# A hybrid recurrent trunk on one core: late norm scale, grouped last units, moved output slices, transposed scan outputs

## What is computed

```python
def rmsnorm(x, w):
    return x * rsqrt(mean(x * x) + EPS) * w
def swiglu(h, wg, wu, wd):
    return (silu(h @ wg) * (h @ wu)) @ wd
# state space scan of a chunk, for head r of group g
acs = cumsum(ac)
lmat = where(causal, exp(acs_i - acs_j), 0)
y = einsum('bijg,bijgr,bjgrp->bigrp', c @ b.T, lmat, xs * dt)
y = y + einsum('bign,bgrpn->bigrp', cc, S) * exp(acs)
S = S * exp(acs[-1]) + einsum('bjgn,bjgr,bjgrp->bgrpn', bc, exp(acs[-1] - acs), xs * dt)
y = y + xs * d_skip
```

## Time and profile before

| | |
|---|---|
| median of three runs | 3383.99 us (3383.58 to 3386.05) |
| the profiled execution | 3374.13 us |
| its span | 3372.3 us |
| TensorE busy | 3171.9 us, 94% |
| VectorE, ScalarE, GpSimd busy | 1592.2, 782.3, 1006.2 us |
| mean granted clock of TensorE | 0.987 of 2.4 GHz |

### The profile page before, as it was taken

How to read it: one execution, slowest core, us unless ns; L and a number is a source line. 1 busy time by engine, 2 the same in 40 slices (tenths; PEclk the granted TensorE clock), 3 DMA queues, 4 the chain that set the end, 5 groups by cost and what they waited for, 6 DMA issues and landing times.

```text
span 3372.3 us, 46391 instructions
## 1 busy us (share of the span) xinstructions
PE 3171.9 (94%) x20050; PEld 3047.4 (90%) x20050; DVE 1592.2 (47%) x1899; ACT 782.3 (23%) x1115; POOL 1006.2 (30%) x528
## 2 busy tenths in 40 slices
PE   6999899999799999999897999999978999999997
PEld 5999898888699999999887998989968999999997
DVE  5344647557632222221467858678686221222224
ACT  4222413414410000000134324143244100000002
POOL 2222211201023333332324535344441332333331
PEclk9999999999899999999999999999999999999998
DMA  4111100101011111111112223131220111111111
GB/s 144 65 64 59 53 26 26 46 26 33 20 50 44 51 44 50 44 44 51 39 43 94 79 78 108 57 107 66 88 91 27 53 49 46 44 51 44 51 44 63
DMA packets 79240, 190.79 MB, mean 57 GB/s; under 512 B 20900, under 2 KB 36932, under 8 KB 78920
## 3 DMA queue, kind: packets, MB, share of 16 engines
q1 hardware_dynamic: 52384, 150.03, 13.1%
q10 hardware_dynamic: 26664, 37.88, 3.5%
HBM read 164.07 MB, written 19.59 MB: 54 GB/s over the span
## 4 chain that ended last, share of the span: by engine, by line
PE 82%; DVE 11%; ACT 3%; issue 2%; DMA 1%; ACTq 0%; SPq 0%; DVEq 0%
PE ps_set L555 68%; PE ps_core L815 4%; PE ps_set L564 3%; ACT work L1073 2%; DVE work L1597 2%; PE ps_core L1010 2%; ACT L1073 1%; DVE work L1916 1%; DVE h_lo L1583 1%; PE ps_core L1015 1%; DVE work L1807 1%; DVE work L2127 1%; PE ps_core L1005 1%; DVE work L2079 1%; DMA x<-in_x 1%
## 5 line engine op out<-in xcount | busy, mean ns | idle before, releaser
L481 POOL CAST w_hi<-w_raw 128x1024 fp32r<-128x1024 f32 x230 | 260.0, 1130 | 2185.7 <-PE ps_set L555 1949.9
L555 PE MATMUL ps_set<-h_hi,w_hi 128*128 128x344 f32 x3696 | 812.5, 328 | 14.6 <-ACT work L1073 14.5
L555 PE MATMUL ps_set<-h_lo,w_hi 128*128 128x344 f32 x3696 | 784.5, 320 | 0.0
L555 PE MATMUL ps_set<-h_hi,w_lo 128*128 128x344 f32 x3696 | 780.9, 320 | 0.0
L555 PEld LDWEIGHTS ps_set<-h_hi,w_hi 128*128 128x128 f32 x3696 | 620.6, 188 | 37.7 <-issue 17.1
L555 PEld LDWEIGHTS ps_set<-h_lo,w_hi 128*128 128x128 f32 x3696 | 625.2, 189 | 0.0
L555 PEld LDWEIGHTS ps_set<-h_hi,w_lo 128*128 128x128 f32 x3696 | 616.7, 188 | 0.0
L484 POOL TENSOR_TENSOR w_lo<-w_raw,w_hi 128x1024 fp32r<-128x1024 f32 x230 | 597.8, 2599 | 18.4
L2014 DVE TENSOR_TENSOR work<-work,ps_set 128x1032 f32<-128x1032 f32 x44 | 54.1, 1229 | 816.2 <-PE ps_set L555 806.3
L1672 DVE TENSOR_TENSOR x<-x,ps_set 128x1032 f32<-128x1032 f32 x160 | 196.7, 1229 | 256.4 <-PE ps_set L555 256.4
L1073 ACT ACTIVATE work<-ps_set 128x1032 f32<-128x1032 f32 x116 | 120.1, 1035 | 721.5 <-PE ps_set L555 695.0
(11 more groups left out here) (224 smaller groups left out, 3427.8 us busy)
## 6 DMA issues: line engine op xcount, KB each, us to landing
w_raw<-in_w SPq DMA_DIRECT2D x230, 512.0 KB, 3.3
work<-ssm_cum_rows ACTq DMA_DIRECT2D x32, 512.0 KB, 4.1
sample<-in_ssm_state SPq DMA_DIRECT2D x16, 512.0 KB, 4.0
out_ssm_s<-sample SPq DMA_DIRECT2D x16, 512.0 KB, 2.6
x<-in_x SPq DMA_DIRECT2D x6, 688.0 KB, 14.8
work<-work ACTq DMA_DIRECT2D x16, 258.0 KB, 2.4
out_y<-x SPq DMA_DIRECT2D x6, 688.0 KB, 3.4
sample<-bc_rows SPq DMA_DIRECT2D x8, 512.0 KB, 4.8
```

Source lines behind the costliest of these rows:

```text
L481: return nc.gpsimd.tensor_copy(w_hi[:, k, :], w_raw[:, k, :])
L555: mm = nc.tensor.matmul(out[:, g, 0:TN], w[:, slot, cols], v[:, g * TN:(g + 1) * TN], start=(start and n == 0), stop=(stop and n == 2))
```

## The change

Four changes stand in one kernel.

1. Norms 1 and 3 give x times w without the root. VectorE multiplies the gate by the root as it leaves PSUM, ScalarE takes its Silu, VectorE multiplies that by the root again (for the up side) and then with the up unit. The mean squares move behind projections.
2. Tile B of every pair is multiplied, copied and subtracted by token groups, and the last up unit of each feed-forward part is projected by groups.
3. In the last delta head, seven of eight output slices of the head before, and the additions to x, move from the levels to ahead of u and into the recurrence.
4. In the scan y comes out channels by tokens: the operands of yc and y are swapped, so that the y products have 64 columns of weights and write one half of the partitions each. The factor exp(cum) is then a row by tokens (`ECUM`), broadcast by two more DMAs of ScalarE for a chunk and exponentiated there. Both scalings of x read PSUM (dt goes into KDEC once). The product is added to the carried part, then D times x (`skip`). The transposes of y go.

```diff
@@ boundary on TensorE
+                if n in (1, 3):
+                    for g in range(TG):
+                        outputs_of(g)
+                    projections(0)
+                    mean_square(0)
+                    projections(1)
+                    mean_square(1)
+                    projections(2, lambda: mean_square(2))
+                    return
@@ gated_delta on TensorE
-                fill(out, 1)
+                fill(out, 0 if h + 1 == HEADS else 1)
+
+                late = h + 1 == HEADS
...
-                        fill(out, 1)
+                        if not late:
+                            fill(out, 1)
...
+                if late:
+                    fill(out, 1)
                 pe.wait_ge(*gdn_dve.value(n("Nb")))
...
+                    if late and c < 6:
+                        fill(out, 1)
@@ ffn on TensorE
+                def by_group(jobs, job, turn, unit):
+                    part = take(jobs, job, turn)
+                    pe.wait_ge(w_split, unit + 1)
+                    for g in range(TG):
+                        for c in range(KC):
+                            mm = group_products(ps_set[part][:, g, :], unit % 2, c, (h_hi[:, c, :], h_lo[:, c, :]), g,
+                                                c == 0, c == KC - 1)
+                        mm.then_inc(*((unit_done, 1) if g == TG - 1 else (part_done, 1)))
@@ state_space on TensorE
-                        nc.tensor.matmul(ps_core[part][:, :], tok(5, c * P, c * P + P), work[:, 12, 0:512],
-                                         start=True, stop=True).then_inc(*ssm_pe.step(n(f"yc{c}")))
+                        for t in range(4):
+                            mm = nc.tensor.matmul(ps_core[part][:, t * P:(t + 1) * P], work[:, 12, t * P:(t + 1) * P],
+                                                  tok(5, c * P, c * P + P), start=True, stop=True)
+                        mm.then_inc(*ssm_pe.step(n(f"yc{c}")))
...
-                        mm = nc.tensor.matmul(ps_core[part][:, h * HD:(h + 1) * HD], SC_TILE[c % 2][:, h],
-                                              XDT[c % 2][:, h * HD:(h + 1) * HD], start=True, stop=True)
+                        lower = HD * (h % 2)
+                        mm = nc.tensor.matmul(ps_core[part][lower:lower + HD, h // 2 * P:(h // 2 + 1) * P],
+                                              XDT[c % 2][:, h * HD:(h + 1) * HD], SC_TILE[c % 2][:, h], start=True, stop=True)
...
-                    part = take(core, n(f"yt{c}"), 0, [n(f"y{c}")])
-                    for t in range(4):
-                        mm = nc.tensor.transpose(ps_core[part][:, t * P:(t + 1) * P], work[:, 11, t * P:(t + 1) * P], ident)
-                    mm.then_inc(*ssm_pe.step(n(f"yt{c}")))
@@ ScalarE
+                def products(g, first=0, last=KC):
+                    for c in range(first, last):
+                        if c % 2 == 0:
+                            act.wait_ge(*x_pair_ready(n, g, c // 2))
+                        fn(h_hi[:, c, span(g)], x[:, c, span(g)], ACT.Identity, scale=NORM_W[:, n, c:c + 1])\
+                            .then_inc(*norm_act[n].step(f"hi{c}.{g}"))
...
+                    fn(RSTD, RSTD, ACT.Exp, scale=-0.5).then_inc(*norm_act[n].step("rstd"))
...
+            def end_rows(c, gr):
+
+                if c > 2:
+                    act.wait_ge(*ssm_dve.value(f"acc{c - 2}.{gr}"))
+                heads = ssm_cum_rows[gr][c].rearrange("(t e n) -> t e n", e=2, n=P)
+                for e in range(2):
+                    act.dma_start(ECUM[c % 2][HD * e:HD * e + HD, :].rearrange("p (t n) -> p t n", n=P),
+                                  heads[:, e, :].unsqueeze(0).to_broadcast([HD, 4, P])).then_inc(ecum_in[c % 2], 16)
...
                     if c:
+                        end_rows(c, gr)
                         differences(c, gr)
                         decays(c, gr)
+                        act.wait_ge(ecum_in[c % 2], 32 * ((4 if c % 2 else 3) * gr + (c + 1) // 2))
+                        fn(ECUM[c % 2], ECUM[c % 2], ACT.Exp).then_inc(*ssm_act.step(n(f"ec{c}")))
@@ VectorE
+                if n == 1:
+                    for g in range(TG):
+                        for q in range(4):
+                            add(g, q)
+                    lows(0, 0, KC)
+                    lows(1, 0, KC)
+                    sums(0)
+                    lows(2, 0, KC)
+                    sums(1)
+                    sums(2)
+                    return
...
+                    v.tensor_tensor(grp(tok(c)), grp(RSTD), big(jobs.part(name)), ALU.mult).then_inc(jobs.sem(name), 1)
+                    dve.wait_ge(*ffn_act[m].value("silu" + "AB"[c], pair))
+                    v.tensor_tensor(tok(c), tok(c), RSTD, ALU.mult).then_inc(*ffn_dve[m].step("f" + "AB"[c]))
...
+                    if last and c < 6:
+                        add_before(c + 2)
...
+                    turned = heads8(ps_core[core.part(n(f"xt{c}"))][:, :])
+                    v.tensor_tensor(heads8(XDT[s]), turned, spread(dt, HD), ALU.mult)
+                    v.tensor_tensor(heads8(XDEC[s]), turned, spread(KDEC[:, c, mine], HD), ALU.mult)\
                         .then_inc(core.sem(n(f"xt{c}")), 1)
...
+                        end = ECUM[c % 2]
                         dve.wait_ge(*ssm_pe.value(n(f"yc{c}")))
...
+                        dve.wait_ge(*ssm_act.value(n(f"ec{c}")))
+                        v.tensor_tensor(end, end, ps_core[core.part(n(f"yc{c}"))][:, :], ALU.mult).then_inc(core.sem(n(f"yc{c}")), 1)
...
+                        v.tensor_tensor(end, end, ps_core[core.part(n(f"y{c}"))][:, :], ALU.add).then_inc(core.sem(n(f"y{c}")), 1)
...
+                    if c:
+                        dve.wait_ge(*core.read(n(f"y{c}")))
+                        skip(end).then_inc(*ssm_dve.step(n(f"acc{c}")))
```

More of the change, by code:

```diff
@@ new lines, in pair @@
+                def pair(i, k, last=False):
+                    unit = i * 12 + (base + 4 + 6 * k)
+                    count = i * 2 + (k + 1)
+                    gate(loop, f"ga.{k}", i, unit, 0, count, i * 2 + k)
+                    gated_a(loop, f"ua.{k}", i, unit + 1, count)
+                    add_outputs(loop, [f"out{t}.{k}" for t in range(KC)], i, unit + 2, i * 12 + (parts + 6 * k))
+                    low_a(count)
+                    gate(loop, f"gb.{k}", i, unit + 4, 1, count, i * 2 + k)
+                    gated_b(loop, f"ub.{k}", i, unit + 5, count, last)
```

228 lines of the change are left out of this document (152 added, 76 removed).

## The result

The changed kernel takes 3389.65 us (median of 20 runs, 3385.78 to 3396.78) where the kernel before, timed beside it, takes 3384.36 (20 runs, 3380.58 to 3387.63): ratio 1.0018, 95% interval 1.0011 to 1.0025. Slower by 5 us, where 3325.5 was predicted and 3297 to 3358 was the range.

The account below looks back on a forecast made before the run. TensorE was taken to bound the kernel, hardly waiting in the feed-forward loops, with idle time that could go in six places. 11 + 11 + 13 + 1.5 + 22 = 58.5 us off the median 3384.0 gave 3325.5 us, range 3297 to 3358.

Parts of the forecast that it names:

- Part 4: State space scan: without y transposes a chunk takes 9.1 us, 0.87 less; 22 us gained over four groups, ends 0 and 38.
- D times x 1.04: Scan, VectorE's work for a chunk: multiplying x by D and adding was put at 1.04 us.
- VectorE's ring: Scan: VectorE's chain of work from one yc to the next, 8.9 us a chunk, 9.2 with the sum over samples.
- Rival (a): Scan: its wait comes back in full because VectorE, stretched by GpSimd, needs 9.9 us a chunk; gain 36.5, 3347; chance 0.17.
- Rival (b): Scan: even and odd heads' y products run at once on array halves, y 1.0 us; 27 us more, 3298; chance 0.10.
- Part 1: Norms 1 and 3: projections start before the root is ready; 11 us gained at boundary 1 and 11 at boundary 3.
- the one load for both: Boundaries: one table set holding logarithm and exponential would give 2.6 us more; the sum kept the second load, 1.28 us.
- two bank waits cost 2 us: Boundary 3: VectorE's additions and lows beside the outputs make two bank waits costing 2 us; gain still 11 us.
- Part 2: Ends of both feed-forward parts: working by groups removes 4.7 us of wait and some 1.8 of low clock; 13 us together.
- Part 3: Last delta head: levels and the stretch ahead of u gain, recurrence loses 7.7 us; net gain 1.5 us, ends -6 and +7.
- rival (d): Scan: added broadcasts delay the row broadcast on ScalarE's queue; chunk 11.7 us, +56 for the scan, 3404; chance 0.03.
- ScalarE's ring: Scan: landing 4.1 us plus 3.5 us of differences and exponential, 7.6 us; covered except 1.5 us at the fourth chunk.

## Why the prediction was wrong

**Part 4, the step that failed.** "D times x 1.04" in VectorE's ring took the 341 ns of L2127 in the earlier trace rows, an instruction that reads PSUM, for one that reads SBUF twice. The two sizes are equal; the operand's place is not. It measured 1255 ns in 64 of 112, 58 us. The earlier trace rows had the warning: of the 128x512 instructions L2062 and L2105, both inputs in SBUF, took 988 and 1246 ns, and L2102, from PSUM, 689. I had even used that difference once, as a gain, for the second scaling, and didn't apply it to the edit that went the other way. How far this step reaches: with the sum in PSUM or one wide addition at the end the kernel gets 27 or 32 us back, of the 47 that lie between the forecast -22 and the measured +25. The new scan then gains 2 or 7 us over the old one (0.9939 or 0.9923 against 0.9944, with intervals that overlap), not 22. The rest is a bank held longer in the one, and waits that are left in the other; no run splits it further.

The Trainium skill (SBUF — State Buffer, Who interferes with whom) states the rule: a VectorE instruction with two SBUF inputs contends with a GpSimd instruction that reads SBUF, and whichever started first holds the shared ports for its whole length while the other is blocked. The trace agrees: each of four short instructions ends 0.14 or 0.15 us behind one of GpSimd's, as above, and with GpSimd idle each takes 0.34 us. I left this rule out of the prediction; it was the one that spoke against the change. An estimate from the traces' own durations (four instructions, each behind one of GpSimd's 2.4 to 2.7 us, in three chunks of eight) gives up to 10 us a chunk, tens of microseconds over the scans.

**Rival (a) was the nearest.** It named VectorE, stretched by GpSimd. I argued against it with VectorE's idle time of 7.3 us a group. But that idle time was the room in which the stretching was free, and the change spent it: the two kernels without the sample work say that this work, with its waits and its sums, costs the old scan 6 us (1 - 0.9983) and the new one 76 (1.0018 - 0.9792). Its price, the wait back in full, was no upper bound. Where it said 3347, the kernel took 3389.65.

**Rival (b) came true in its mechanism.** The y products take 1.09 us for 16, not 2.05; a chunk without slow instructions takes 8.83 us, against 9.1 forecast. In the changed kernel without the sample work a group of the scan, from its first y product to that of the next group, takes 196.5 us as a mean, in the kernel before without the same work 206.1: 9.6 less, beyond the 5.5 forecast. With all of the work it is 214.9 in the changed kernel against 207.1 before. By the Trainium skill (TensorEngine Tiling (Array Packing), Overview and Key Properties) tiles of 64 columns may run in parallel, up to twice as fast, and a change of mode drains the engine. The trace agrees with the first, 1.09 us against the 2.05 that 16 products at the pace of 128 by 128 take. Of the second it shows next to nothing: the eight products ahead of them start 1.08 us before the first, where at 0.123 each they need 0.98.

**Part 1.** Boundary 1 gave 9.1 of 11: right. The two waits on a low were 1.69 and 1.80 us. The table load between logarithm and exponential was there, 1.28 us at 937.99, so the one load for both of the Trainium skill (ScalarE: Activation LUTs, Table sets: the hidden batching unit) is not what the trace shows, and its 2.6 us didn't come. The added work on VectorE was undercounted, 84 us in the first feed-forward loop (162.2 to 246.4), so 7.7 us a pair instead of 3.7. It was free all the same: TensorE is busy in all of the loop's 704.26 us. Boundary 3 gave 2.8 of 11. The step that failed is "two bank waits cost 2 us": its durations came from the earlier trace rows, stretches with GpSimd idle, and beside GpSimd's lows an addition of 1.23 us takes 3.44. In the changed kernel TensorE waits 2.40 us for a bank there and 3.08 us for the first sum of squares. Without most of GpSimd's lows the first is gone and the stretch takes 79.1 us, 10.9 below that of the kernel before, which had them; the second stays, and its cause is open.

**Part 2.** Forecast 13 for both ends, measured 4.8 + 4.9 = 9.7, within its ends 9 to 14. The wait fell from 4.74 to 1.32, not to nothing.

**Part 3.** The recurrence step is 3.65 us as forecast (867.17 - 863.52), and the levels lost their slices. Two terms were mis-sized. From the start of level 1 to the last products of the levels the head gained 4.4 us (41.8 to 37.5), where 6.8, less 0 to 2 for the clock, were forecast; most of what is missing is the clock: 48 products took 7.46 us instead of 5.9, with the granted clock at 0.61 over 4 us. From the end of u to the outputs of the boundary it lost 9.5 us (27.5 to 37.0), where 7.7 were forecast. Sum +1.5 in the trace instead of -1.5.

**The whole.** Parts 1 to 3: 19 to 20 of 36.5 us. Part 4: 25 us lost, 22 forecast as a gain. ScalarE's ring, rival (d), was not the main bound: the row broadcast landed in 3.6 to 5.6 us and the added ones in 2.9 to 7.2, median 3.5, and the operand's place alone took 27 us away. It isn't nothing either: VectorE's idle time ahead of the scores, which ScalarE ends, grew over the four scans from 1.9 to 13.9 us (25.2 without the sample work), where 1.5 us a group, 6 in all, were allowed for it. No run isolates it. What stays open besides: how much of the new scan's loss is the waiting itself and how much the lower clock after it; no run separated these.

## What to carry to other kernels

When an edit moves an operand of a VectorE instruction from PSUM to SBUF, price it from a row with both inputs in SBUF and GpSimd busy, and count instructions, not bytes: here each of four short ones waited for one of GpSimd's, and one wide one in their place waited 1.2 us as a mean. An engine's idle time is where its stretched instructions are free; before taking that idle time, ask what it was hiding. Where an operand can stay in PSUM without holding a bank that others wait for, leave it there while GpSimd works, and give the unavoidable SBUF pair to one wide instruction.

## What the runs showed of the hardware

A 128x128 VectorE instruction with two SBUF inputs took 0.34 us alone and up to 2.58 beside GpSimd's of 2.4 to 2.9 us; four in a row each ended 0.14 or 0.15 us behind one of four GpSimd instructions, one of them a copy of 1.10 us with a single input in SBUF. With one input in PSUM, 128 of them took 0.337 us as a mean beside the same work. Cutting GpSimd's instructions from 1024 to 256 columns brought the mean from 1255 to 597 ns, and cost GpSimd 3.56 us for 2.60 (measured in the kernel before). Products with 64-column weights that go to alternate halves took 1.09 us for 16 of 128 columns, 0.068 us each, where products with 128-column weights take 0.123.
